# Output projection of a decoder layer as seven block products, with summed weight blocks and part of their splitting on GpSimd

## What is computed

```python
merged = g_nsa * (o_nsa @ w_branch_nsa[l]) + g_sgu * (o_sgu @ w_branch_sgu[l])
mix = merged @ w_out[l]                                   # 512x1024 by 1024x1024
h = layer_norm(DEEPNORM_ALPHA * h + mix, ln1_g[l], ln1_b[l])
ffn = (jax.nn.silu(h @ w_ffn_gate[l]) * (h @ w_ffn_up[l])) @ w_ffn_down[l]
h = layer_norm(DEEPNORM_ALPHA * h + ffn, ln2_g[l], ln2_b[l])
```

## Time and profile before

| | us |
|---|---|
| median of 3 runs | 714.79 (714.63 to 715.0) |
| the profiled execution | 714.27 |
| its span, first to last instruction | 712.5 |
| TensorE busy | 700.1 (98%) |
| VectorE busy | 567.7 (80%) |
| ScalarE busy | 352.3 (49%) |
| GpSimd busy | 151.4 (21%) |

### The profile page before, as it was taken

One profiled execution on the slowest core, in us unless ns is written; L12 is line 12 of the kernel. 1 busy time (PEld: TensorE's weight loads), 2 busy tenths in 40 slices (PEclk: granted clock), 3 DMA queues, 4 the chain that ended last, 5 costly groups with the idle time before them and its releaser, 6 DMA issues.

```text
span 712.5 us, 11496 instructions
## 1 busy us (share of the span) xinstructions
PE 700.1 (98%) x4232; PEld 622.8 (87%) x4232; DVE 567.7 (80%) x918; ACT 352.3 (49%) x552; POOL 151.4 (21%) x167
## 2 busy tenths in 40 slices
PE   8999999999999999999999999999999999999995
PEld 7888988878888988888899899999999998888885
DVE  6985499787778784675889588899898886977877
ACT  6462777467777778322524244444444344145600
POOL 2942960422132210000000222222222210000001
PEclk9999999999999999999999999999999999999999
DMA  8712343111101205536522143233233328500102
GB/s 317 229 43 68 110 119 119 60 59 60 33 28 60 59 1 147 208 119 232 160 82 61 58 118 97 80 118 118 67 110 118 114 74 301 194 26 0 60 31 88
DMA packets 55716, 73.84 MB, mean 104 GB/s; under 512 B 4096, under 2 KB 40704, under 8 KB 55552
## 3 DMA queue, kind: packets, MB, share of 16 engines
q1 hardware_dynamic: 55392, 72.19, 31.1%
q0 software_dynamic: 144, 1.05, 0.7%
q10 hardware_dynamic: 144, 0.13, 0.1%
HBM read 70.21 MB, written 2.10 MB: 101 GB/s over the span
## 4 chain that ended last, share of the span: by engine, by line
PE 91%; DVE 5%; ACT 1%; issue 1%; DMA 0%; DVEq 0%; SPq 0%; ACTq 0%
PE ps L1979 61%; PE ps L2428 10%; PE ps L2062 5%; PE ps L2446 5%; PE ps L1991 3%; PE ps L1987 2%; PE ps L1988 2%; DVE wl L1250 1%; PE ps L2001 1%; DVE prob L1531 1%; ACT prob L1011 1%; DVE ptl L1250 1%; DMA stage<-in_w_in 0%; PE ps L2419 0%; DVE vstat L1384 0%
## 5 line engine op out<-in xcount | busy, mean ns | idle before, releaser
L1979 PE MATMUL ps<-xh,wh 128*128 128x256 f32 (+1 forms) x416 | 135.0, 325 | 0.0
L1979 PE MATMUL ps<-xh,wl 128*128 128x256 f32 (+1 forms) x416 | 131.7, 317 | 0.0
L1979 PE MATMUL ps<-xl,wh 128*128 128x256 f32 (+1 forms) x416 | 131.6, 316 | 0.0
L1979 PE MATMUL ps<-ath,wh 128*128 128x256 f32 (+1 forms) x280 | 86.1, 307 | 0.0
L1979 PE MATMUL ps<-ath,wl 128*128 128x256 f32 (+1 forms) x280 | 86.0, 307 | 0.0
L1979 PE MATMUL ps<-atl,wh 128*128 128x256 f32 (+1 forms) x280 | 86.0, 307 | 0.0
L1979 PEld LDWEIGHTS ps<-xh,wl 128*128 128x128 f32 x416 | 79.3, 191 | 5.4
L1979 PEld LDWEIGHTS ps<-xh,wh 128*128 128x128 f32 x416 | 79.5, 191 | 3.2
L1979 PEld LDWEIGHTS ps<-xl,wh 128*128 128x128 f32 x416 | 79.5, 191 | 3.1
L1250 DVE TENSOR_TENSOR wl<-stage,wh 128x512 fp32r<-128x512 f32 (+2 forms) x73 | 64.6, 897 | 4.9 <-ACT wh L794 2.6
L1240 DVE TENSOR_TENSOR wl<-stage,wh 128x2048 fp32r<-128x2048 f32 (+1 forms) x19 | 43.1, 2266 | 27.6 <-ACT wh L791 19.4
(11 more groups left out here) (374 smaller groups left out, 1741.6 us busy)
## 6 DMA issues: line engine op xcount, KB each, us to landing
stage<-in_w_ffn_gate SPq DMA_DIRECT2D x22, 512.0 KB, 4.8
stage<-in_w_ffn_up SPq DMA_DIRECT2D x22, 512.0 KB, 4.6
stage<-in_w_in SPq DMA_DIRECT2D x20, 512.0 KB, 4.2
stage<-in_w_ffn_down SPq DMA_DIRECT2D x14, 512.0 KB, 4.1
quad_raw<-in_w_in SPq DMA_DIRECT2D x8, 512.0 KB, 9.4
stage<-in_w_out SPq DMA_DIRECT2D x8, 512.0 KB, 4.7
quad_raw<-in_w_ffn_down SPq DMA_DIRECT2D x4, 1024.0 KB, 11.1
arena<-in_x_t SPq DMA_DIRECT2D x8, 256.0 KB, 5.8
```

What stands on the lines that cost most here:

```text
L1979: return pe.matmul(out, (sh, sh, sl)[i], (mh, ml, mh)[i], start=start and i == 0, stop=stop and i == 2)
```

## The change

With A the merged activations and W the weights, both cut into 2x2 blocks (token half by feature half, feature half by column half), the 8 block products become 7, each on 256 tokens, 512 features and 512 columns: 24 matmuls instead of the old 192 in all, so 168. They use the activation blocks A(0,0), A(0,1), A(1,1) and four sums of blocks, and the weight blocks W(0,0), W(1,0), W(1,1) and four sums of blocks.

- Weight sums: SP loads a raw block, and GpSimd issues a transfer from DRAM that adds a second block onto it (`more_rows`, five of them, 1 MB each, one after the other by `more_in`).
- Activation sums: three on VectorE (`out_s`), one on GpSimd. Each is then rounded on ScalarE (`out_s_hi`) and its low half taken on VectorE (`out_s_lo`).
- Low halves of the weight blocks: four on VectorE (`out_t_lo`), three on GpSimd (`out_lo`, 128x2048 each), and the low half of the first FFN weights, `first_l`, also moves from VectorE to GpSimd. Weight slots: `wh`/`wl` 0 and 1 and, as third, the upper half of `ath`/`atl`.
- The PSUM banks of a product go into `y` by `take`, with + or -, on 256 tokens at a time; the first product is also copied out by ScalarE.
- The first norms now run on tiles 0 and 1 after the sixth product's operands are made, and on tiles 2 and 3 after the seventh product.

In the diff below `P1` to `P7` of the text are the seven `out_product` calls in their order; `U_OUT` units vanish.

```diff
+        def merged(half, k_half):
+            return x_block(merge, half, k_half)
+
+        def spare(at):
+            return arena[:, at:at + 1024].rearrange("p (k n) -> p k n", n=256)
+
+        m_t, m_b = arena[:, 8192:10240], arena[:, 4096:6144]
+        first_product = fact[:, 8:10, :]
+        M_S = {"s1": spare(6144), "s2": spare(7168), "s3": s1,
+               "s4": fact[:, 10:12, :].rearrange("p f (h n) -> p (f h) n", n=256)}
+        M_S_AT = {"s2": (1, 0), "s1": (0, 0), "s4": (0, 1), "s3": (1, 0)}
+        M_SLOT = ([(wh[:, b, :], wl[:, b, :]) for b in range(2)] +
+                  [(ath[:, 2048:4096], atl[:, 2048:4096])])
...
+            sp.wait_ge(st_done, 4)
+            out_rows(m_t, 1, 1, 0)
...
-            with sp.Fori(0, 2) as c:
-                for kh in range(2):
-                    load(2 * c + U_OUT + kh, kh, rows4(wout_d, kh, kh, 512 * c, 512))
-
+            sp.wait_ge(w_lo, U_BRANCH + 3)
+            out_rows(stage[0][:, :], 0, 0, 1)
+            sp.wait_ge(mg_ok, 4)
+            out_rows(m_b, 1, 0, 2)
+            sp.wait_ge(w_lo, U_BRANCH + 4)
+            out_rows(stage[1][:, :], 1, 1, 3)
+            sp.wait_ge(part_lo, 9)
+            out_rows(m_b, 0, 1, 2)
+
+            sp.wait_ge(s_sum, 8)
...
+            sp.wait_ge(part_lo, 12)
+            load(U_FFN, 0, rows8(gate_d, 0, 0))
+            sp.wait_ge(pool_lo, 1)
+            load(U_FFN + 1, 1, rows8(up_d, 1, 0))
...
+            def more_rows(n, dst, k_half, half, q, count):
+
+                pool.wait_ge(raw_arrived[q], count)
+                if n:
+                    pool.wait_ge(more_in, 16 * n)
+                pool.dma_start(dst.rearrange("p (k n) -> p k n", k=4),
+                               wout_d[:, 4 * k_half:4 * k_half + 4, 512 * half:512 * half + 512],
+                               accum_op=ALU.add).then_inc(more_in, 16)
+
+            def out_lo(slot, raw_t, hi_count):
+                pool.wait_ge(part_hi, hi_count)
+                h, l = M_SLOT[slot]
+                pool.tensor_tensor(l, raw_t, h.bitcast(fp32), ALU.subtract).then_inc(pool_lo, 1)
+
+            more_rows(0, m_t, 0, 1, 0, 64)
+            more_rows(1, m_t, 0, 0, 0, 64)
+            pool.wait_ge(part_lo, 10)
+            more_rows(2, stage[0][:, :], 0, 1, 1, 64)
+            more_rows(3, m_b, 1, 1, 2, 96)
+            pool.wait_ge(mg_lo, KD)
+            pool.wait_ge(s_sum, 7)
+            pool.tensor_tensor(M_S["s4"], merged(0, 1), M_S["s2"], ALU.add).then_inc(s_sum, 1)
+            pool.wait_ge(part_lo, 11)
+            more_rows(4, m_t, 1, 0, 0, 64)
+            out_lo(2, stage[1][:, :], 13)
+            out_lo(1, m_b, 14)
+            out_lo(0, m_t, 15)
+            pool.wait_ge(w_hi, U_FFN + 1)
+            pool.tensor_tensor(first_l[:, :], stage[0][:, :], first_h[:, :].bitcast(fp32), ALU.subtract).then_inc(w_lo, 1)
...
+            out_t_hi(2, m_b, arrived_in=(2, 64))
+            act.wait_ge(w_used, U_BRANCH + 3)
+            out_t_hi(0, stage[0][:, :], arrived_in=(1, 64))
+            for f in range(4, 7):
+                merged_hi(f)
+            act.wait_ge(w_used, U_BRANCH + 4)
+            out_t_hi(1, m_t, 2)
+            merged_hi(7)
+            act.wait_ge(in_used, 8)
+            act.copy(first_product, ps[:, 0:2, :]).then_inc(bank_out, 1)
+            out_s_hi("s2", 7)
+            out_s_hi("s1", 6)
+            out_t_hi(0, stage[0][:, :], 3)
+            out_t_hi(2, stage[1][:, :], arrived_in=(3, 64), used=9)
+            out_s_hi("s4", 8)
+            out_t_hi(1, m_b, 4, used=10)
+            out_s_hi("s3", 5)
+            split_to(first_h[:, :], U_FFN, 0, U_FFN)
+            out_t_hi(0, m_t, 5, used=11)
...
+            dve.wait_ge(sig_ok, 2)
+            for f in range(4):
+                gated(0, f, 0)
+            split(U_BRANCH + 2, 0)
+            for f in range(4):
+                merged_sum(0, f)
+                merged_lo(f)
+            dve.wait_ge(mg_ok, 4)
+            out_s(5, "s3", merged(0, 0), merged(1, 0))
+            split(U_BRANCH + 3, 1)
+            dve.wait_ge(sig_ok, 4)
+            for f in range(3):
+                gated(1, f, 0)
+            out_t_lo(2, m_b, 9)
+            gated(1, 3, 0)
+            out_t_lo(0, stage[0][:, :], 10)
+            for f in range(3):
+                merged_sum(1, f)
+                merged_lo(4 + f)
+            merged_sum(1, 3)
+            dve.wait_ge(mg_ok, KD)
+            out_s(6, "s1", merged(1, 0), merged(1, 1))
+            merged_lo(7)
+            out_s(7, "s2", M_S["s1"], merged(0, 0))
+            out_t_lo(1, m_t, 11)
+            out_s_lo("s2", 13)
+            out_s_lo("s1", 14)
+            out_t_lo(0, stage[0][:, :], 12)
...
+            dve.wait_ge(in_used, 9)
+            take(5, 0, 0, b_banks, ALU.add, True)
+            out_s_lo("s4", 15)
+            dve.wait_ge(in_used, 10)
+            take(6, 0, 1, a_banks, ALU.subtract, True)
+            dve.wait_ge(bank_out, 5)
+            take(7, 0, 0, first_product, ALU.add)
+            dve.wait_ge(in_out, 7)
+            moments(0, 0)
+            moments(1, 0)
+            out_s_lo("s3", 16)
+            dve.wait_ge(in_used, 11)
+            take(8, 2, 1, b_banks, ALU.add, True)
+            take(9, 0, 1, b_banks, ALU.add)
+            dve.wait_ge(ln_arrived, 64)
+            for m in range(2):
+                if m:
+                    dve.wait_ge(in_used, 12)
                 else:
-                    dve.wait_ge(w_used, U_OUT + 2)
-                add_rows(m, 0, m).then_inc(mg_lo, 1)
-                dve.wait_ge(mg_lo, KD + m + 1)
-                moments(m, 0)
-            split(U_OUT + 3, 1)
-            split_to(first_l[:, :], first_h[:, :], U_FFN, 0)
-            dve.wait_ge(ln_arrived, 64)
-            for m in range(MT):
-                if m < 3:
-                    dve.wait_ge(rows_done, 12 + m + 1)
-                else:
-                    dve.wait_ge(w_used, U_FFN)
-                add_rows(m, 1, m).then_inc(mg_lo, 1)
-                dve.wait_ge(mg_lo, KD + MT + m + 1)
+                    dve.wait_ge(rows_done, 10)
+                take(10 + m, m, 1, ps[:, 4 + m:5 + m, :], ALU.add)
+                dve.wait_ge(in_out, 10 + m)
                 step(moments(m, 1))
                 variance(m)
                 norm(m)
-                if m == 1:
-                    ht_lo_of(0)
+            dve.wait_ge(in_used, 13)
+            take(12, 2, 1, a_banks, ALU.subtract)
+            take(13, 2, 0, a_banks, ALU.add, True)
+            ht_lo_of(0)
+            ht_lo_of(1)
+            dve.wait_ge(in_out, 12)
+            for m in (2, 3):
+                moments(m, 1)
+            for m in (2, 3):
+                if m == 3:
+                    dve.wait_ge(in_used, 14)
+                else:
+                    dve.wait_ge(rows_done, 11)
+                take(12 + m, m, 0, ps[:, m:m + 1, :], ALU.add)
+                dve.wait_ge(in_out, 12 + m)
+                step(moments(m, 0))
+                variance(m)
+                norm(m)
...
-            def last_rows(m, kh):
-                tok = slice(P * m, P * m + P)
-                if kh == 0:
-                    pe.wait_ge(mg_lo, KD + m + 1)
-                for k in range(4):
-                    last = mm3(ps[:, m, :], xh[:, 4 * kh + k, tok], xl[:, 4 * kh + k, tok], w4(wh, kh)[:, k, :],
-                               w4(wl, kh)[:, k, :], kh == 0 and k == 0, kh == 1 and k == 3)
-                if m == MT - 1:
-                    last.then_inc(w_used, 1)
-                elif kh == 1:
-                    last.then_inc(rows_done, 1)
-
-            pe.wait_ge(w_lo, U_OUT + 3)
-            last_rows(0, 0)
-            last_rows(1, 0)
-            pe.wait_ge(w_lo, U_OUT + 4)
-            last_rows(0, 1)
-            last_rows(1, 1)
-            last_rows(2, 0)
...
+            pe.wait_ge(mg_lo, 4)
+            pe.wait_ge(br_prod, 16)
+            pe.wait_ge(part_lo, 10)
+            out_product(0, (0, 0), 0, True).then_inc(in_used, 1)
+            out_product(2, (0, 1), 2, True, by_k=True).then_inc(in_used, 1)
+            pe.wait_ge(part_lo, 11)
+            pe.wait_ge(xt_lo, 13)
+            pe.wait_ge(bank_out, 5)
+            out_product(1, M_S_AT["s2"], 0, False).then_inc(in_used, 1)
+            pe.wait_ge(part_lo, 12)
+            pe.wait_ge(xt_lo, 14)
+            pe.wait_ge(in_out, 5)
+            out_product(0, M_S_AT["s1"], 2, True).then_inc(in_used, 1)
+            pe.wait_ge(pool_lo, 1)
+            pe.wait_ge(xt_lo, 15)
+            out_product(2, M_S_AT["s4"], 4, True, (0,)).then_inc(rows_done, 1)
+            out_product(2, M_S_AT["s4"], 4, True, (1,)).then_inc(in_used, 1)
+            pe.wait_ge(pool_lo, 2)
+            pe.wait_ge(xt_lo, 16)
+            pe.wait_ge(in_out, 6)
+            out_product(1, M_S_AT["s3"], 0, False).then_inc(in_used, 1)
+            pe.wait_ge(pool_lo, 3)
+            pe.wait_ge(in_out, 11)
             h_transposed(0)
-            last_rows(2, 1)
-            last_rows(3, 0)
```

(5 more changed lines are left out.)

161 lines of the change are left out of this document (97 added, 64 removed).

## The result

The changed kernel took 730.05 us (median of 728.76, 729.32, 730.77 and an execution of 1402.86 that is far off the others and left out of the ratio; the median of the other three is 729.32) against 714.71 before (714.79 without its fourth execution): 1.0209 of it, interval 1.0194 to 1.0224, so about 15 us slower. Its profiled execution took 730.77 with a span of 728.8.

The account below looks back on a forecast made before the run. TensorE was taken as the bound; 24 fewer matmuls save 5.44 us, but stalls behind VectorE, blocked by GpSimd, net +10.0 to +12.0. The middle, +11.0 on 714.27, gives 725.3, plus 0.52 for the median 725.8; range 715.3 to 731.5.

Parts of the forecast that it names:

- main case: GpSimd's subtractions block VectorE for the whole instruction, delaying the last first tile by +11; range 722.5 to 728, chance 0.55.
- P1's stall: Before the first product, TensorE waits 3.85 us for VectorE's last gate product; 2.7 to 5.9 as ends.
- P1 to P5 otherwise without a wait: First five products run 5.44 us in all, to 348.2, operands in time; accumulating transfers 7.6 us each.
- The blocking: VectorE instructions with two SBUF inputs wait until GpSimd's 4.61-us subtraction ends: 3.7 us for s4's low half, 3.4 next.
- (b): FFN weights late, s3 first, P6 on time; `first_l` inside tile 0's norm, transpose stalls 8.5 us; +12.0 in all.
- (a): GpSimd's third low half precedes s3: P6 stalls 3.45 us, the transpose of tile 0 3.2; +10.0 in all.
- The VectorE-bound rest: From tile 0's transpose on, VectorE is slower than TensorE, giving stalls of 0.9, 1.1 and 3.5 us.
- The sign of being wrong that came true: In the profile after, a clock below 1.00 following TensorE's stalls would show the forecast wrong.
- rival 4: Clock falls in the stalls: P1 costs 5.4 more, a first tile 2.8; 728.6 to 734.0; chance 0.10.
- rival 1: Little or no blocking, VectorE's chain alone decides: +1.4 to about +4.5, 716.2 to 719.3; chance 0.16.
- Rival 2: Faster: blocking misses TensorE, only P1's 3.85 stands against 5.44 us of matmuls saved; 713.2; chance 0.12.
- rival 3: Accumulating transfers are the bound: 12 us each give +13.3, 13 +15.9, 15 +22; 728 to 737; chance 0.07.

Follow-up runs that it names:

- The two runs on reading and writing: Against the changed kernel, GpSimd's four subtractions cut to 128x8 columns: 720.98 us; replaced by equally long zero fills that read no SBUF: 721.28 us.
- the last version without fillers: Changed kernel with `first_l` subtracted after tile 1's norm and ScalarE's root for tile 3 ahead of the next weights, no extra TensorE matmuls: 724.19 us.
- The run without subtractions and with fillers: Changed kernel with GpSimd's four subtractions cut to 128x8 columns and unread matmuls put in TensorE's waits: 721.08 us, ratio 1.0093.

## Why the prediction was right

The forecast was 725.8, slower; measured were 730.05, slower and inside the range (715.3 to 731.5), some 4 us above the forecast. It lies above the main case's own range (722.5 to 728): the mechanism and the places of the waits came as forecast, and the number is still inside only by the room that the range left at the top for the late weights and the clock.

- **P1's stall**: forecast 3.85, measured 3.18; its start 322.21 - 1.89 = 320.3 on the clock of before against 321.0.
- **P1 to P5 otherwise without a wait**: right. The five accumulating transfers were costed too low (7.6 us each; the page of after has 12.8 as the median of four, and all five lie between 8.5 and 15.6), and so was their issue on GpSimd (1.06 each as an upper price; 1.27 to 1.49 measured), but the time to spare covered that:

```profile
arena<-in_w_out POOLq DMA_DIRECT2D x4, 1024.0 KB, 12.8
```

- **GpSimd's subtraction**: estimated 4.61 from two shorter shapes, measured 4.61 to 4.75.
- **The blocking**: VectorE's low half of s4 forecast to wait 3.7 us, measured 4.80 - 1.23 = 3.6; the addition of the copied product 3.4, measured 3.1. The two runs on reading and writing show the mechanism itself.
- **The two cases for the third low half**: (b) came true. The FFN weights landed late (ScalarE rounds them at 348.23, and the block for the third low half behind them at 350.05), s3's low half went first, `first_l` fell into the norm of tile 0, and the transpose of tile 0 stalled 8.0 us against 8.5. (a), which would have given 1 us less than the middle that I took, is out.
- **The VectorE-bound rest**: 0.9 and 1.1 us were forecast before the transpose of tile 1 and the first FFN tile; the trace has neither, since TensorE ran at the lower clock there and used them up. 3.5 forecast before the transpose of tile 2, measured 3.25.
- **The sign of being wrong that came true**: the prediction named three, and one of them, a clock below 1.00 after the stalls, is in the rows of after (0.50 to 0.63). GpSimd and VectorE side by side at full speed, and TensorE waiting for GpSimd or a transfer, are not.
- **The mis-sized term is the clock**: I had it at nothing in the sum and as a rival at 0.10. It is not a rival but an addition: it falls after each of the three waits, and where rival 4 gave 5.4 us for P1 and 2.8 for a tile at half speed, it measured 1.7 and 1.4, since the full clock came back within each. Only the last of the three reaches the end. The sum (b), +12.0, with 1.4 for it makes 13.4; measured between the same places 14.4; of the missing 1.0 some 0.6 were there at the transpose of tile 0 already (364.73 - 1.89 = 362.8 against 362.2). The Trainium skill's rule that I weighed there ("TensorE: Matmul & The Clock Gate", section Part 1: The HAM clock gate: an idle array is set to the lower clock, and gets the full one back after a stretch of work) agrees with the rows of after: 0.50 behind waits of 3.18, 7.99 and 3.25 us, and 1.00 again some us later. The length of the wait alone doesn't settle it: over the runs it fell behind waits from 3.08 us on, yet it stayed at 1.00 behind 3.24 before the transpose of tile 2 with the three low halves on VectorE, and behind 3.63 before P1 in the last version without fillers.
- **Little blocking, faster** (rivals 1 and 2): the cut subtractions give rival 1's number directly. Without blocking the kernel is at 720.98, where that rival had 716.2 to 719.3; its clock falls as well, which the rival left out. Rival 2 is out with it: even without blocking the kernel is slower than before.
- **Late accumulations** (rival 3): its condition came true, 12 us and more for a transfer, and its +13.3 to +15.9 for 12 to 13 us happens to hold the measured 14.4. But the run with the subtractions cut has transfers just as long (12.4 as the median of four on its page) and is at 720.98, so they are not what the blocking cost.

What stays open is what the remaining 6 us are. P1's late start and VectorE's chain from norm 1 to norm 2 are two parts. A third, in the trace of the run with the subtractions cut, is a wait of VectorE in the middle of the norm of tile 0:

```profile
351.00 0.16 DVE L1769 RECIPROCAL nrm<-nrm 128x1 f32<-128x1 f32 x1 [3.56 <-ACT nrm L1157]
```

It waits for ScalarE's root, which stands in ScalarE's list behind the rounding of the first FFN weights, and that waited for their load:

```profile
345.74 1.91 ACT L1127 CAST first_h<-stage 128x2048 fp32r<-128x2048 f32 x1 [5.91 <-DMA stage<-in_w_ffn_gate]
```

The run without subtractions and with fillers has the same wait, 3.65 us. So the rest isn't VectorE's own chain alone, as that run's expectation had it; by estimate up to some 3.5 us of it may hang on a transfer and on ScalarE's order ahead of that root, which no run here changed. Nor is there one without both P1's wait and the blocking: the run that took P1's wait away did so with the blocking in place, where it could show nothing.
